# Grouped attention steps taken tile by tile, with both heads' work of a kind side by side

## What is computed

```python
def gqa_attention(q, k, v):
    scale = HEAD_DIM ** -0.5
    def block(qb):
        s = jnp.einsum('bqkgd,bskd->bkgqs', qb, k).astype(jnp.float32) * scale
        p = jax.nn.softmax(s, axis=-1).astype(v.dtype)
        return jnp.einsum('bkgqs,bskd->bqkgd', p, v)
    return from_blocks(lax.map(block, to_blocks(q)))

# encoder_layer
o_g = gqa_attention(q_g, k_g, v_g).reshape(B, S, GQA_Q)
x = x + jnp.concatenate([o_g, o_d], axis=-1) @ w_out
```

## Time and profile before

| what | value |
|---|---|
| median of 3 runs | 1852.48 us (1852.32, 1852.48, 1856.47) |
| profiled execution, own time | 1850.91 us |
| span of that execution | 1849.0 us |
| PE busy | 1766.7 us, 96% |
| PEld busy | 1553.7 us, 84% |
| DVE busy | 1177.3 us, 64% |
| ACT busy | 807.6 us, 44% |
| POOL busy | 239.8 us, 13% |
| mean granted TensorE clock | 0.992 |

### The profile page before, as it was taken

One profiled execution on the slowest core, in us unless ns is written; L12 is line 12 of the kernel. 1 busy time (PEld: TensorE's weight loads), 2 busy tenths in 40 slices (PEclk: granted clock), 3 DMA queues, 4 the chain that ended last, 5 costly groups with the idle time before them and its releaser, 6 DMA issues.

```text
span 1849.0 us, 28540 instructions
## 1 busy us (share of the span) xinstructions
PE 1766.7 (96%) x11280; PEld 1553.7 (84%) x11280; DVE 1177.3 (64%) x1955; ACT 807.6 (44%) x1771; POOL 239.8 (13%) x351
## 2 busy tenths in 40 slices
PE   5999999998999999999999999999899999999998
PEld 5888777778999999999888877777789898989896
DVE  4655887775756565656565368786766565656564
ACT  4323777744333333333332348775534242424242
POOL 2301423231000000000012014231500000000000
PEclk9999999999999999999999999999999999999999
DMA  4221000102231313131222110002022222222222
GB/s 158 64 66 55 17 9 13 58 23 69 58 92 46 92 46 92 46 92 46 69 67 60 58 35 25 1 24 69 1 80 69 68 69 69 70 69 70 68 80 79
DMA packets 121907, 108.19 MB, mean 59 GB/s; under 512 B 3472, under 2 KB 95760, under 8 KB 121776
## 3 DMA queue, kind: packets, MB, share of 16 engines
q1 hardware_dynamic: 120096, 100.74, 18.2%
q0 software_dynamic: 960, 3.28, 0.6%
q10 hardware_dynamic: 720, 2.36, 0.3%
HBM read 103.22 MB, written 3.15 MB: 58 GB/s over the span
## 4 chain that ended last, share of the span: by engine, by line
PE 85%; DVE 6%; ACT 4%; issue 2%; POOL 1%; DMA 1%; SPq 0%; POOLq 0%; ACTq 0%; DVEq 0%
PE bank L1670 15%; PE bank L1672 14%; PE bank L1671 14%; PE bank L1986 11%; PE bank L1990 11%; PE bank L1988 11%; PE bank L1762 4%; PE bank L1753 3%; ACT stage L952 1%; PE bank L1905 1%; DVE neg_max L1358 1%; PE bank L1711 1%; ACT stage L972 1%; POOL hrstd L609 1%; DMA x<-in_x_prompt_dram 1%
## 5 line engine op out<-in xcount | busy, mean ns | idle before, releaser
L1670 PE MATMUL bank<-w_hi,hT_hi 128*128 128x512 f32 (+1 forms) x624 | 245.5, 393 | 11.6 <-DVE hT_lo L1394 4.6
L1672 PE MATMUL bank<-w_hi,hT_lo 128*128 128x512 f32 (+1 forms) x624 | 234.9, 376 | 0.0
L1671 PE MATMUL bank<-w_lo,hT_hi 128*128 128x512 f32 (+1 forms) x624 | 234.2, 375 | 0.0
L1254 DVE TENSOR_TENSOR x<-x,bank 128x512 f32<-128x512 f32 x120 | 81.2, 686 | 119.4 <-PE bank L1672 118.9
L1670 PEld LDWEIGHTS bank<-w_hi,hT_hi 128*128 128x128 f32 x624 | 118.3, 190 | 42.0 <-issue 10.8
L607 POOL TENSOR_TENSOR ms<-ss,eps_col 128x1 f32<-128x1 f32 x30 | 6.5, 216 | 1065.4 <-ACT headsq L800 1065.4
L1672 PEld LDWEIGHTS bank<-w_hi,hT_lo 128*128 128x128 f32 x624 | 118.3, 190 | 21.8
L1986 PE MATMUL bank<-hT_hi,w_hi 128*128 128x384 f32 x368 | 124.9, 339 | 8.8 <-issue 5.0
L1671 PEld LDWEIGHTS bank<-w_lo,hT_hi 128*128 128x128 f32 x624 | 118.7, 190 | 17.2
L1990 PE MATMUL bank<-hT_hi,w_lo 128*128 128x384 f32 x368 | 124.4, 338 | 0.0
L1988 PE MATMUL bank<-hT_lo,w_hi 128*128 128x384 f32 x368 | 124.3, 338 | 0.0
(11 more groups left out here) (213 smaller groups left out, 4586.3 us busy)
## 6 DMA issues: line engine op xcount, KB each, us to landing
x_raw<-in_w_gate_up_dram SPq DMA_DIRECT2D x44, 512.0 KB, 5.0
w_raw<-in_w_gate_up_dram SPq DMA_DIRECT2D x44, 512.0 KB, 3.9
w_raw<-in_w_in_dram SPq DMA_DIRECT2D x36, 512.0 KB, 3.7
w_raw<-in_w_down_dram SPq DMA_DIRECT2D x36, 512.0 KB, 3.8
w_raw<-in_w_out_dram SPq DMA_DIRECT2D x16, 512.0 KB, 3.6
x_raw<-in_w_down_dram SPq DMA_DIRECT2D x8, 512.0 KB, 4.2
out_dram<-stage SPq DMA_DIRECT2D x6, 512.0 KB, 2.6
gain<-in_gains_dram POOLq DMA_DIRECT2D x5, 512.0 KB, 4.7
```

The lines of the kernel that those rows point to most:

```text
L1254: dve.tensor_tensor(xs, xs, bank[:, DOWN_BANK[t], :], ALU.add).then_inc(x_added.sem, 1)
L1670: pe.matmul(out, a_hi, b_hi, start=first, stop=False)
L1671: pe.matmul(out, a_hi, b_lo, start=False, stop=False)
L1672: return pe.matmul(out, a_lo, b_hi, start=False, stop=last)
```

## The change

In a grouped step, PE now issues the scores of `e+2` first, then both heads' products of `e-1`, then both heads' transposes of `e`, then the mix transposes. ACT issues both exponentials of `e+1` first, then both high parts, then the mix high. DVE issues the maximum of `e+2` first, takes the product of `e-1` (with one more wait, on its own inverse sums), then both low parts, mix low and inverse sums. What is left over after the last step is both products of the last tile on PE, and no low part on DVE. No instruction on data is added or removed, and the differential steps stay.

```diff
@@ ACT
             def grouped_step(l, e):
                 p, t = divmod(e, T)
-                probT_high(l, e, t, 0, 0, P_SCALE)
+                for h in range(2):
+                    exp(l, e + 1, (t + 1) % T, h)
+                for h in range(2):
+                    probT_high(l, e, t, h, h, P_SCALE)
                 if mixed_at(e):
                     mixT_high(l, *mixed_at(e), True)
-                for h in range(2):
-                    exp(l, e + 1, (t + 1) % T, h)
-                probT_high(l, e, t, 1, 1, P_SCALE)
@@ DVE
             def take_product(l, e, t):
+                dve.wait_ge(inv_done.sem, inv_done.at(l, e))
                 dve.wait_ge(o_done.sem, o_done.at(l, e))
@@ DVE
             def grouped_step(l, e):
                 p, t = divmod(e, T)
+                row_max(l, e + 2, (t + 2) % T)
                 if e:
-                    probT_low(l, e - 1, (t - 1) % T, 1, 1, P_SCALE)
-                probT_low(l, e, t, 0, 0, P_SCALE)
+                    take_product(l, e - 1, (t - 1) % T)
+                for h in range(2):
+                    probT_low(l, e, t, h, h, P_SCALE)
                 if mixed_at(e):
                     mixT_low(l, *mixed_at(e), True)
-                row_max(l, e + 2, (t + 2) % T)
                 inverse_sums(l, e, t)
-                if e:
-                    take_product(l, e - 1, (t - 1) % T)
@@ DVE, after the grouped steps
-                probT_low(l, GROUPED - 1, T - 1, 1, 1, P_SCALE)
                 take_product(l, GROUPED - 1, T - 1)
@@ PE
             def grouped_step(l, e):
                 p, t = divmod(e, T)
-                gqa_transpose(l, e, t, 0)
+                scores(l, e + 2, {4: p * 2 + 2, 0: p * 2 + 1}.get(t))
+                if e:
+                    for h in range(2):
+                        grouped_product(l, e - 1, h)
+                for h in range(2):
+                    gqa_transpose(l, e, t, h)
                 if mixed_at(e):
                     transpose_mix(l, *mixed_at(e), True)
-                scores(l, e + 2, {4: p * 2 + 2, 0: p * 2 + 1}.get(t))
-                if e:
-                    grouped_product(l, e - 1, 1)
-                gqa_transpose(l, e, t, 1)
-                grouped_product(l, e, 0)
@@ PE, after the grouped steps
-                grouped_product(l, GROUPED - 1, 1)
+                for h in range(2):
+                    grouped_product(l, GROUPED - 1, h)
```

## The result

The changed kernel takes 1869.76 us (median of 4 runs, 1868.24 to 1873.68), the kernel before 1852.40 us beside it (median of 4, 1847.98 to 1856.47). The ratio is 1.0094, with a 95% interval of 1.0073 to 1.0115: slower, by 17.4 us. The forecast was 1868 and "slower".

What follows compares the result with a forecast made beforehand. PE was taken as the bound of the grouped steps, DVE close behind. Added waits of 11.04 us less 3.05 taken away gave +8.0 us a layer, +16.0 in all: 1868 us, range 1857 to 1880.

Steps and rivals of the forecast that it cites:

- The chain: Grouped steps: PE transposes, ACT high part, DVE low part, PE product; left uncovered, it adds waits of 11.04 us a layer.
- The chain of a plain 4-block tile: From the start of head 0's transposes to its product, without the mix: 2.06 us.
- The waits: PE ahead of products, chain less cover: tiles 2 and 5 0.15, tile 4 0.49, tile 3 1.19, tile 1 0.60 us.
- The end: Last tile of a layer, no scores behind its transposes: its product waits 2.06 - 0.91 = 1.15 us.
- the second heads' 0.02: Head 1's product at each 4-block tile waits 0.02 us more, 16 times a layer: 0.32 us.
- the lap check: Cross-check over six tiles: 16.54 - 0.18 + 2.58 + 0.08 = 19.0 us against 17.23, +1.8 a lap, 7.1 a layer.
- The start: PE's first work, now scores, waits for both exponentials: about half a microsecond to either side, taken as zero.
- What was taken away: On PE, fewer turns 0.7, no late mix transposes 1.5, no left-over product wait 0.83: 3.05 us a layer.
- The added wait ahead of the take: On DVE, for its own sums of the step before, long done: costed at nothing, otherwise 1.2 us a layer.
- The clock rival: New PE gaps make the granted clock fall at each of eight tile-3 waits: 13.6 us on top, 1882; chance 0.13.
- The no-change rival: Mix low parts do not hold products of tiles 3 and 1: only +2.4 us a layer, 1857; chance 0.08.
- The faster rival: Chain and cover meet at PE's wait for head 0's low part: 6.1 us gained, 1846; chance 0.05.

Runs made afterwards that it cites:

- e3: Changed kernel with ACT making head 0's high part of every grouped tile twice, the extra copy to an unread buffer: 1889.85 us (one run).
- e5: Changed kernel with PE's transposes ahead of the previous tile's products, a second buffer for odd tiles' turned probabilities, DVE's take last: 1844.77 us, ratio 0.9972.
- e6: Changed kernel with PE's transposes ahead of the previous tile's products and a second buffer, but DVE's take second, ahead of the low parts: 1874.19 us, ratio 1.0129.
- e4: Kernel before with ACT making head 0's high part of every grouped tile twice, the extra copy to an unread buffer: 1860.36 us (one run).
- e7: Changed kernel's order on PE alone, with ACT and DVE ordered as in the kernel before: 1933.41 us (one run).
- e1: Changed kernel with mix transposes, mix high and mix low moved ahead of the tile's own parts on PE, ACT and DVE: 1860.37 us, ratio 1.0034.
- e2: Kernel before with both products issued a tile later, behind the next tile's transposes and scores, and a second buffer for odd tiles: 1848.64 us, ratio 0.9976.

## Why the prediction was right, step by step

- **The chain was the cause.** e3 shows it on the path at each tile. e5 shows that cover takes the loss away, with the same pieces in the same number; it does so only with the take moved behind the low parts, since the same cover with the take ahead of them (e6) is slower than the changed kernel. The order of the losses over the tiles came as forecast: tile 3 most, then tiles 1 and 4, tiles 2 and 5 little, tile 0 none.
- **The chain of a plain 4-block tile was mis-sized by 0.08.** From a tile's transposes to its product it is 230.98 - 228.84 = 2.14 (tile 4) and 223.49 - 221.35 = 2.14 (tile 2), against 2.06. The chain of work of the changed kernel shows in which piece (first what follows the mix's low part at tile 3, then tile 4):

```profile
227.59 0.09 issue
...
229.51 0.61 ACT stage L972
...
230.14 0.70 DVE stage L1384
230.84 0.14 issue
```

The high part starts 0.67 after the transposes (228.84 to 229.51; 0.68 was forecast), high 0.61, low 0.70 and their hand-overs are as the rows of before gave them. It is PE's pick-up after the low part: 0.14 here, where the row that I took it from had 0.04 to 0.06. The same place in the chain of work of the kernel before, behind the low part of 263.39:

```profile
264.09 0.04 issue
```

The place of before is a product of head 1, which in the program waits for its low part alone; a product of head 0 waits for other things first, and stands behind scores or transposes and not behind a product. In e4, too, it is 0.05 at that left-over product and 0.14 at products of head 0. Which of the two differences makes it no run tells.
- **The waits, by distance.** A wait is the chain less the cover, both as distances between starts. Tile 4: 2.14 - (229.84 - 228.84) - 0.56 = 0.58, forecast 0.49. Tiles 2 and 5: 0.24, forecast 0.15. Tile 3: (227.68 - 224.66) - (225.88 - 224.66) - 0.56 = 1.24, forecast 1.19; its chain was 3.02 against 3.00, the two low parts and the mix low in a row as worked out. Tile 1: (220.77 - 219.24) - 0.90 = 0.63, forecast 0.60. The end: 2.14 - 0.91 = 1.23, forecast 1.15. A lap thus waits 2.93, against 2.58.
- **What was forecast too high** made up for part of that: the second heads' 0.02 was nothing, since the 40 matmuls of both heads run as one row, 223.49 to 224.66, 1.17 us, as two of 0.58 would. By the lap check, 16.54 - 0.18 + 2.93 = 19.29, and 19.27 was measured (19.0 forecast).
- **The layer** then comes out at four laps of +2.04, less 0.33 for tile 1, whose wait now (0.63) and before (0.30) is missing in the first lap, nothing at the end (1.23 in place of 0.24 and 1.00: by distance, 264.14 - 262.56 - 0.58, the wait of before was 1.00 and not the 0.83 that its row shows), +0.46 at the start, where PE's first work waits 4.11 and not 3.65, and +0.08 ahead of the differential work: 8.4, with 8.35 and 7.85 measured and 8.0 forecast. The start, which I had taken as nothing within half a microsecond, was at the dear end.
- **What was taken away** was mis-sized, and here luck helped. No mix transpose waits and the turns are gone, as forecast; the sum priced that at 0.18 + 0.45 = 0.63 a lap. Measured it is 17.23 - (19.27 - 2.93) = 0.89, since the 0.2 us of a lap that the prediction could not place went too. The sum's 2.58 + 0.08 - 0.63 = +2.03 a lap thus meets the measured +2.04 with two errors of 0.27 and 0.26 against each other. The lap check had the 0.89 nearly right and came out at +1.8, because of its shorter waits.
- **The added wait ahead of the take** was rightly costed at nothing: in the first layer nine of the 24 takes show idle time of DVE before them, each ended by PE's product (0.32 to 0.91 us).
- **The clock rival** fell for the laps: clock 1.00 over 78.4 us in both layers, with gaps of 1.18 and 0.51 in each lap. Falls inside the laps do occur, in e7: there, with PE idle 0.84 to 2.03 us ahead of the scores, the clock was 0.50 for 6.7 us. The Trainium skill, "TensorE: Matmul & The Clock Gate", section "A second HAM failure mode: psum-queue depth-cycling", tells of a kernel in which frequent short idling between groups of matmuls makes the clock swing; e7 agrees, and the changed kernel shows gaps of the same kind that did not do it. Right behind the second stage the changed kernel has a fall that the kernel before has not; it is worth 1.5 us.
- **The no-change rival** named the right part and too large a share: with the mix out of the way (e1) the kernel is at 1860.4 us, +0.34%, and not at 1857. The mix transposes no longer lengthen tile 3's cover either, so it waits 0.51, not 0.25.
- **The faster rival** was right on what is there to gain (1846 forecast, 1844.77 in e5), and on the condition: chain and cover must meet. It is reached by more cover, not by a shorter chain, and with the mix's low part still in its place.

A version that beats both kernels is e5: PE in the order scores, transposes, mix, products of the tile before; a second buffer for the turned probabilities; the take last on DVE.

## What to carry to other kernels

Where one engine bounds and its result goes through two other engines back to it, add up that chain once and the bound engine's work between its two ends once, tile by tile; the difference is the loss, and putting like work side by side takes cover away unless a second buffer lets another tile's work stand in between. On an in-order engine look for loops: an instruction that waits for the bound engine must not stand ahead of one that the bound engine waits for. Read waits as distances between starts, since the idle time in brackets leaves out some of it.

## What the runs showed of the hardware

- The idle time shown before a waiting product is less than what the wait cost by distance: 0.51 against 0.58, 0.17 against 0.24, 1.18 against 1.24, 1.07 against 1.23. The row ahead ends in the profile after the next group could have started: at tile 4 the scores end at 230.18 + 0.28 = 230.46, and by distances between starts the product could have come at 229.84 + 0.56 = 230.40.
- PE picked up a finished low part after 0.04 to 0.05 us at the left-over product of head 1 (the kernel before, e4) and after 0.09 to 0.14 in other places.
- A row of eight transposes that starts behind a wait of 0.58 us was 1.22 us long in e6; behind a product, without a wait, it is 1.07 (the changed kernel).
- The granted clock stayed at 1.00 through waits of 1.18 and 0.51 us in each 19.3 us, and fell to 0.50 in e7.
- The same gap did not always bring the clock down. Behind PE's 2.28 to 2.37 us of idle time ahead of the differential work it fell behind both stages in the profiled executions of the changed kernel, e2, e3 and e6, behind one of the two in the kernel before and e4, and behind neither in e1, e5 and e7. A fall cost 1.5 us by distance in the changed kernel, so two executions can differ by some 3 us by this alone, as an estimate.
